# Modulation products of a two-block transformer kernel on four column positions at once

## The reference

```
c_act = silu(c)                                   # 1 x 2048
for l in range(2):
    mod = c_act @ w_mod[l] + b_mod[l]             # w_mod[l]: 2048 x 6144
    shift, scale, gate = split(mod, 3)
    h = rmsnorm(x, norm_gain[l]) * (1 + scale) + shift
    proj = h @ w_in[l]                            # 2048 x 7504
    ...                                           # sparse attention, retention, gates
    x = x + gate * (y @ w_out[l])                 # 2048 x 2048
```

## Time and profile before

| | |
|---|---|
| median of three runs | 3432.7 us |
| profiled execution | 3433.9 us, span 3432.1 us |
| TensorE matmuls | 2305.4 us busy, 67% |
| VectorE (DVE) | 1783.1 us, 52% |
| ScalarE (ACT) | 884.2 us, 26% |
| DMA | 900.92 MB, mean 262 GB/s |
| w_mod loads | 192 of 512 KB, median 4.6 us from issue to landing |
| modulation matmuls | 768, mean 671 ns, from 15.4 to 700.4 us |
| first piece of layer 0, last gate group stored | 153.85 us, 700.07 us |
| first piece of layer 1 | 824.58 us |

### The profile page before, as it was taken

One profiled execution on the slowest core, in us unless ns is written; L12 is line 12 of the kernel. 1 busy time (PEld: TensorE's weight loads), 2 busy tenths in 40 slices (PEclk: granted clock), 3 DMA queues, 4 the chain that ended last, 5 costly groups with the idle time before them and its releaser, 6 DMA issues.

```text
span 3432.1 us, 29641 instructions
## 1 busy us (share of the span) xinstructions
PE 2305.4 (67%) x11714; PEld 1506.5 (44%) x11714; DVE 1783.1 (52%) x2738; ACT 884.2 (26%) x1322; POOL 724.6 (21%) x552
## 2 busy tenths in 40 slices
PE   5899999988999878998998888123322322232235
PEld 1366666567878666665666678100000000000001
DVE  2324545655566765433234557955655565555440
ACT  1133443343455344354354442000000000000000
POOL 1000000000000000000000002555555555555552
PEclk9899999999999999999999999656666666666567
DMA  7787776744655443533332467799999999999998
GB/s 244 255 270 233 246 229 214 239 158 139 181 160 150 146 132 118 150 114 105 92 99 85 142 184 283 305 421 421 421 422 421 421 422 422 422 421 422 421 422 348
DMA packets 268133, 900.92 MB, mean 262 GB/s; under 512 B 20358, under 2 KB 45196, under 8 KB 201548
## 3 DMA queue, kind: packets, MB, share of 16 engines
q0 software_dynamic: 75776, 545.73, 38.6%
q1 hardware_dynamic: 191776, 352.69, 33.0%
q10 hardware_dynamic: 444, 0.61, 0.1%
HBM read 894.77 MB, written 2.10 MB: 261 GB/s over the span
## 4 chain that ended last, share of the span: by engine, by line
PE 55%; DMA 28%; DVE 10%; ACT 3%; issue 2%; POOL 1%; SPq 0%; DVEq 0%; POOLq 0%; ACTq 0%
PE pp L1635 47%; DMA late<-in_peer_v,MI 9%; PE tp L1635 6%; DMA P<-in_peer_v,MI 4%; DMA ring<-in_peer_v,MI 4%; DMA x<-in_peer_v,MI 4%; DMA ring<-in_w_mod 2%; DVE wL L997 2%; DMA SY<-in_peer_v,MI 2%; PE tp L1638 2%; DVE P L1050 2%; DMA ring<-in_peer_w_query 1%; DMA ring<-in_w_in 1%; ACT wH L518 1%; DVE P L1594 0%
## 5 line engine op out<-in xcount | busy, mean ns | idle before, releaser
L997 DVE TENSOR_TENSOR wL<-ring,wH 128x1024 fp32r<-128x1024 f32 (+3 forms) x504 | 581.6, 1160 | 649.7 <-ACT wH L518 648.9
L1635 PE MATMUL pp<-wH,hH 128*128 128x512 f32 (+3 forms) x1888 | 752.0, 398 | 52.6 <-issue 17.9
L1635 PE MATMUL pp<-wL,hH 128*128 128x512 f32 (+3 forms) x1888 | 719.6, 381 | 0.0
L1635 PE MATMUL pp<-wH,hL 128*128 128x512 f32 (+3 forms) x1888 | 719.5, 381 | 0.0
L518 ACT ACTIVATE wH<-ring 128x1024 fp32r<-128x1024 f32 (+3 forms) x504 | 503.5, 1005 | 551.3 <-PE pp L1635 340.1
L1635 PEld LDWEIGHTS pp<-wH,hH 128*128 128x128 f32 x1888 | 360.2, 191 | 263.9 <-issue 149.0
L1635 PE MATMUL pp<-late,S 128*32 128x512 f32 x736 | 229.7, 893 | 296.7 <-DMA P<-in_peer_v,MI 76.0
L1635 PEld LDWEIGHTS pp<-wH,hL 128*128 128x128 f32 x1888 | 360.0, 191 | 64.2
L1635 PEld LDWEIGHTS pp<-wL,hH 128*128 128x128 f32 x1888 | 360.9, 191 | 54.6 <-issue 0.5
L1635 PE MATMUL pp<-P,S 128*32 128x512 f32 x376 | 265.3, 872 | 146.8 <-DMA x<-in_peer_v,MI 73.8
L1635 PE MATMUL pp<-x,S 128*32 128x512 f32 x376 | 165.6, 874 | 223.8 <-DMA ring<-in_peer_v,MI 223.8
(11 more groups left out here) (296 smaller groups left out, 3020.4 us busy)
## 6 DMA issues: line engine op xcount, KB each, us to landing
ring<-in_w_in SPq DMA_DIRECT2D x288, 512.0 KB, 3.8
ring<-in_w_mod SPq DMA_DIRECT2D x192, 512.0 KB, 4.6
ring<-in_w_out SPq DMA_DIRECT2D x96, 512.0 KB, 4.6
ring<-in_w_in SPq DMA_DIRECT2D x48, 368.0 KB, 3.8
ring<-in_peer_w_query SPq DMA_DIRECT2D x32, 512.0 KB, 4.8
ring<-in_w_in SPq DMA_DIRECT2D x24, 344.0 KB, 3.1
ring<-in_w_in SPq DMA_DIRECT2D x16, 256.0 KB, 3.6
U<-in_dm POOLq DMA_DIRECT2D x8, 384.0 KB, 4.3
```

What stands on the lines that cost most here:

```text
L997: tt(lo, raw, hi.bitcast(F32), ALU.subtract).then_inc(*tick("dve_lo", *names))
L1635: return e.matmul(o, l, r, start=start, stop=stop, skip_group_check=skip)
```

## The change

- A w_mod load is 128 rows by 1024 columns (512 KB as before, rows of 4 KB). TensorE makes four products of 256 columns of it, one for each column position; the position stands for a quarter of the columns, and all sixteen row blocks are added up in place. A block of 1024 columns takes sixteen loads.
- The loads have buffers of their own. In the lead (loads 0 to 63) there are eight, in `late`; after it (64 to 191) two, in the columns of `P` that hold the gates later. Eight, or two, loads are issued ahead; load m + 8 or m + 2 waits for the use of m. Load 64 also waits until the last chunk of the hidden state is turned. ACT's store of the first gate group waits for the use of load 191. The ring serves the other weights alone.
- The sums: ACT copies 256 columns, TensorE turns them with two products against a four-column `ROW`, and DVE adds the bias straight from PSUM; `mrow` is gone. It is done once for 1024 columns, twelve times in all instead of 24.
- The M lane of the 128 later loads is opened after group 0 of layer 0 instead of ahead of it, and its rate in the projections is 1.5 steps a piece instead of 1.0: one and two steps in turn.

```diff
-    cw[:, ROW] = (i % 32) == 0
+    cw[:, ROW:ROW + 4] = i[:, None] == 32 * np.arange(4)[None, :]
...
-    yield "open", "M", "mods", 0, 0, 8
+    yield "open", "M", "mods", 0, 4
...
-    yield "open", "M", "mods", 0, 8, 12
-    yield "open", "M", "mods", 1, 0, 8
-    yield "open", "M", "mods", 1, 8, 12
...
         def after_in(n):
+            if n == 0 and l == 0:
+                yield "open", "M", "mods", 4, 12
...
-        yield from project(2 * l, after_in, lambda n: (0.7 if n < 14 else 1.0, 0.6, 1.0))
+        yield from project(2 * l, after_in, lambda n: (0.7 if n < 14 else 1.0, 0.6, 1.5))
...
+        mod_in = [*[late[:, 1024 * b:1024 * b + 1024] for b in range(8)], P[:, 0, GA:GA + 1024], P[:, 1, GA:GA + 1024]]
...
+        def mod_slot(m):
+
+            if m < 64:
+                return m % 8, m - 8 if m >= 8 else None
+            return 8 + m % 2, m - 2 if m >= 66 else None
...
-            def mods(l, g0, g1):
-                for g in range(g0, g1):
-                    for pc in range(8):
-                        load(I["w_mod"][l, pc * 256:(pc + 1) * 256, g * 512:(g + 1) * 512]
-                             .rearrange("(k p) n -> p k n", p=128), 2, 512)
-                        if pc < 7:
-                            yield
-                    yield
+            def mod_load(m):
+                block, k = m // 16, m % 16
+                l, c0 = block // 6, block % 6 * 1024
+                b, before = mod_slot(m)
+                if before is not None:
+                    w.wait_ge(*at("mod used", before))
+                if m == 64:
+                    w.wait_ge(*at("chunk", 0, 3))
+                e.dma_start(mod_in[b], I["w_mod"][l, k * 128:(k + 1) * 128, c0:c0 + 1024]).then_inc(
+                    *landed(f"mod_in{b}", ("mod", m)))
+
+            def mods(b0, b1):
+                first, last, depth = 16 * b0, 16 * b1, 2 if b0 else 8
+                for m in range(first, first + depth):
+                    mod_load(m)
+                for m in range(first, last):
+                    if m + depth < last:
+                        mod_load(m + depth)
+                    if m % 16 < 15:
+                        yield
+                    elif m + 1 < last:
+                        yield
+                yield
...
+                            elif p == 0:
+                                w.wait_ge(*at("mod used", 191))
...
-                    act(msum[:, :], side_bank[:, :], ACT.Copy).then_inc(*tick("act_side", ("side out", s)))
+                    act(msum[:, 0:256], side_bank[:, 0:256], ACT.Copy).then_inc(*tick("act_side", ("side out", n)))
...
-                    copy(mrow[:, 4 * g:4 * g + 4], tp[u % 2][:, 0:4]).then_inc(*tick("dve_side", ("pair free", u)))
...
+                    tt(mc.rearrange("p (g b) -> p b g", g=4), heads(tp[u % 2][:, 0:8], 2),
+                       bcol[:, l * 48 + k0:l * 48 + k0 + 8].rearrange("p (g b) -> p b g", g=4), ALU.add).then_inc(
+                        *tick("dve_side", ("pair free", u)))
...
-                        for k in range(2):
-                            kk = 2 * pc + k
-                            o = 32 * (kk % 4)
-                            m = mm(side_bank[o:o + 32, :], cact[:, kk:kk + 1].to_broadcast([128, 32]), wv[:, k, :], kk < 4, kk >= 12)
...
+                        w.wait_ge(*at("mod", m))
+                        for g in range(4):
+                            z = mm(side_bank[32 * g:32 * g + 32, 0:256], cact[:, k:k + 1].to_broadcast([128, 32]),
+                                   wv[:, 256 * g:256 * g + 256], k == 0, k == 15)
+                        z.then_inc(*tick("pe_side", ("mod used", m), *([("side", n)] if k == 15 else [])))
...
-                    for b in range(4):
-                        m = mm(pr[:, b:b + 1], msum[:, b * 128:(b + 1) * 128], CW[:, ROW:ROW + 1], True, True)
+                    for b in range(2):
+                        z = mm(pr[:, 4 * b:4 * b + 4], msum[:, b * 128:(b + 1) * 128], CW[:, ROW:ROW + 4], True, True)
```

More of the change, by code:

```diff
@@ L334, in mixer_peer_program @@
         mcol = sb("mcol", [128, 2, 48])
-        mrow = sb("mrow", [128, 48])
         msum = sb("msum", [128, 512])
@@ L361, in mixer_peer_program @@
                      "dve_lo", "dve_stored", "dve_x", "dve_y", "dve_h", "dve_side",
-                     "const_in", "pos_in", "x_in", "meta_in", "forget_in", "ffn_in", "decay_in", "turned_in", "out_done",
+                     *[f"mod_in{i}" for i in range(10)], "const_in", "pos_in", "x_in", "meta_in", "forget_in", "ffn_in", "decay_in", "turned_in", "out_done",
                      *[f"ring_in{i}" for i in range(NS)], *[f"expert_in{i}" for i in range(NG)]):
@@ L617, in tables, with mods @@
                             yield
[L619 to L623, removed]
-                            yield
[L625 to L628, removed]
-                    act(msum[:, :], side_bank[:, :], ACT.Copy).then_inc(*tick("act_side", ("side out", s)))
+            def mods(b0, b1):
+                for block in range(b0, b1):
+                    for k in range(16):
+                        if k < 15:
+                            yield
+                    n = next(side)
+                    w.wait_ge(*at("side", n))
+                    if n:
+                        w.wait_ge(*at("side read", n - 1))
+                    act(msum[:, 0:256], side_bank[:, 0:256], ACT.Copy).then_inc(*tick("act_side", ("side out", n)))
                     yield
@@ L1149, in mods @@
                     u = next(turn)
+                    l, k0 = block // 6, block % 6 * 8
+                    mc = mcol[:, l, k0:k0 + 8]
                     w.wait_ge(*at("turned", u))
-                    copy(mrow[:, 4 * g:4 * g + 4], tp[u % 2][:, 0:4]).then_inc(*tick("dve_side", ("pair free", u)))
[L1152 to L1160, removed]
+                    tt(mc.rearrange("p (g b) -> p b g", g=4), heads(tp[u % 2][:, 0:8], 2),
+                       bcol[:, l * 48 + k0:l * 48 + k0 + 8].rearrange("p (g b) -> p b g", g=4), ALU.add).then_inc(
+                        *tick("dve_side", ("pair free", u)))
+                    if block % 6 in (2, 3):
+                        w.wait_ge(*now("dve_side"))
+                        ts(mc, mc, 1.0, None, ALU.add, None).then_inc(*tick("dve_side"))
+                        w.wait_ge(*now("dve_side"))
+                        tt(mc, mc, col("norm_gain", 16 * l + k0 - 16, 8), ALU.mult).then_inc(*tick("dve_side"))
             def meta_sum(p, n):
@@ L1730, in tables, with mods @@
                             yield
[L1732 to L1739, removed]
-                            w.wait_ge(*at("c ready"))
-                            if s:
-                                w.wait_ge(*at("side out", s - 1))
-                        for k in range(2):
-                            kk = 2 * pc + k
-                            o = 32 * (kk % 4)
-                            m = mm(side_bank[o:o + 32, :], cact[:, kk:kk + 1].to_broadcast([128, 32]), wv[:, k, :], kk < 4, kk >= 12)
-                        m.then_inc(*tick("pe_side", ("ring used", r), *([("side", s)] if pc == 7 else [])))
-                        if pc < 7:
+            def mods(b0, b1):
+                for block in range(b0, b1):
+                    n = next(side)
+                    for k in range(16):
+                        m = 16 * block + k
+                        wv = mod_in[mod_slot(m)[0]]
+                        if k == 0:
+                            w.wait_ge(*at("c ready"))
+                            if n:
+                                w.wait_ge(*at("side out", n - 1))
+                        w.wait_ge(*at("mod", m))
[3 more added lines that the diff above has]
+                        z.then_inc(*tick("pe_side", ("mod used", m), *([("side", n)] if k == 15 else [])))
+                        if k < 15:
@@ L1749, in mods @@
                             yield
                     yield
-                    w.wait_ge(*at("side out", s))
+                    w.wait_ge(*at("side out", n))
                     pr, u = pair()
-                    for b in range(4):
-                        m = mm(pr[:, b:b + 1], msum[:, b * 128:(b + 1) * 128], CW[:, ROW:ROW + 1], True, True)
-                    m.then_inc(*tick("pe_turned", ("turned", u), ("side read", s)))
+                    for b in range(2):
+                        z = mm(pr[:, 4 * b:4 * b + 4], msum[:, b * 128:(b + 1) * 128], CW[:, ROW:ROW + 4], True, True)
@@ L1757, in meta_sum @@
+                    z.then_inc(*tick("pe_turned", ("turned", u), ("side read", n)))
             def meta_sum(p, n):
```

## The result

The changed kernel took 3461.6 us (median of four runs, 3460.98 to 3466.65) against 3432.6 us (four runs): a ratio of 1.0073 [1.0060, 1.0087], 0.73% slower. 3391 us was predicted, in a range of 3357 to 3422 us and with a chance of 0.08 for slower. The prediction is wrong in sign, and the time lies outside its range. The profiled execution took 3460.98 us with a span of 3459.1 us, 27.0 us above the span before.

The account below looks back on a forecast made before the run. The lead was taken as bound by a ring too short for the landing time, layer 0's projection by TensorE. Terms -31 - 1 - 5 + 19 - 24 = -42 us took 3433.9 to 3391 us, range 3357 to 3422.

Parts of the forecast that it names:

- The product: TensorE queue: one w_mod load's four-position product costs 0.77 us alone instead of 1.20, 0.43 as second of two.
- The lead: First 64 w_mod loads: eight buffers make DMA engines set the pace at 380 GB/s, x 4 us later; -31 us.
- Turn, group 0, groups 12 to 15: Turn to first piece -1 us; group 0 -5 and groups 12 to 15 -24, as layer 1 without products takes.
- The waits on w_mod: Groups 1 to 11: TensorE waits for loads in two buffers, 27 plus 15 us, 42 in all.
- the product c: Second of two back-to-back products in a two-piece period, following a and b; its load, issued at a's use, comes late.
- The time without waits: Groups 1 to 11: layer 1's 261.9 us plus products and turns of the sums, 350 us against 372.8.
- The landing: SP's w_mod loads: 4.4 us to land by the trace, against a skill-based estimate of 3.2 us.
- So 350 + 42 = 392 us: Groups 1 to 11: work without waits plus waits on w_mod, +19 us against 372.8; bounds -23 and +51.
- The late w_in: Groups 1 to 11: w_in queued behind SP's wait, ready at 7.3 us, needed after 7.7 or more; nothing priced.
- B: Groups 1 to 11: two buffers make landing the bound, 5.7 us or more; stretch +98, 3470 us; chance 0.08.
- A: Groups 1 to 11: loads land in time, under 3.5 us; stretch 350 us, total 3349 us; chance 0.15.
- C: TensorE products: four positions don't help, a load still costs 1.20 us; stretch +57, total 3429 us; chance 0.04.

Follow-up runs that it names:

- experiment 4: Changed kernel, but loads 64 to 191 go through the four ring slots, one a piece, opened ahead of group 0: 3354.8 us, ratio 0.9753.
- Experiment 6: Changed kernel with six buffers for loads 64 to 149 and SP waiting for the product three back: 3359.8 us, ratio 0.9782.
- experiment 7: Changed kernel, still two buffers, but SP waits for the product three back instead of its own step's: 3407.0 us, ratio 0.9911.
- Experiments 1 and 2: Changed kernel with SP's wait one product back (3425.9 us); changed kernel with six buffers for loads 64 to 149, SP's wait unchanged (3442.8 us).
- 9: The kernel of experiment 4 with the load of x issued first in GpSimd's queue, ahead of the constants: 3352.1 us, ratio 0.9748.
- experiment 5: Changed kernel's products and sums, but all 192 loads go through the four ring slots as before the change: 3376.4 us, ratio 0.9824.

## Why the prediction was wrong

**What held.** *The product.* "A single product in the queue then costs 0.77 us": measured 0.75 (experiment 4), with nothing left for an overhead that grows as the columns shrink. The estimate from the Trainium skill, TensorEngine Tiling (Array Packing), section Performance Considerations, would have made it 0.82 us; no such cost is seen. *The lead.* x 3.9 us later (4 said); then 410 GB/s, above my 380 and inside its bounds, at 1.02 DMA share; in exchange a load takes 9.2 us to land, with eight under way. *Turn, group 0, groups 12 to 15* came as derived from the twin. *The waits on w_mod.* 42 us were priced, at the product c, and the matmul queue waits 42.0 us, 36.5 of them at c. That the sums agree so well is partly luck: groups 1 to 3 have 19.6 us of it where 27 were priced, the wide groups 22.4 where 15 were. *The time without waits.* Experiment 6, the same schedule with most of the limits gone, keeps TensorE busy for 348 us at a granted clock of 0.99, against 350 in the sum. *The landing.* The Trainium skill, DMA: Bandwidth & Descriptors, section Anatomy of one DMA, has a fit for GpSimd-issued transfers that gives an estimate of 3.2 us for 512 KB. No w_mod load of the two kernels, all issued by SP, reached it; the shortest took 3.6 us.

**The step that failed: "So 350 + 42 = 392 us" for groups 1 to 11, which leaves two terms at nothing.** It was 477. In the change's own profile the stretch is 348 us of work as experiment 6 has it, 43 us by which the work became longer, 42 us of waits on w_mod, and 43 us of waits for ACT and DVE. The first and the third are the two terms of the sum. The other two are its error.

1. *The late w_in: "It is late only if DVE or ACT is held up; ACT's and DVE's lane work behind it slips along, which the tensor engine then waits for."* The sentence names the mechanism, and the sum gives it nothing. I had worked out the slack of the late w_in for the piece that needs it, 7.3 against 7.7 us, and taken 0.4 us of it as cover. What I left out is what ACT does in order behind its wait for w_in: 43 us of TensorE's idle time, which become 3 us when SP no longer stands in that wait (7). Experiments 1 and 2 show it from both sides: less SP order, more waiting on w_mod, and 40 us gained; hardly any waiting on w_mod, SP's order kept, and only 16 gained.
2. *No price for the clock.* The stretch's 2370 matmuls keep TensorE busy for 348 us in 6, at a granted clock of 0.99; 370 in 7, at 0.95; 392 after the change, at 0.90. The idle time is 20, 55 and 86 us in the three. Of the 708 weight loads for `hH` there, 4, 68 and 103 took over 280 ns, where 188 is usual: so the engine ran at the lower of its two levels, 1.2 instead of 2.4 GHz, for more of the work. 43 of the 109 us between 6 and the change are work that became longer, about 22 in each of the two steps. The Trainium skill, TensorE: Matmul & The Clock Gate, section Part 1 (The HAM clock gate), says that the clock that is let through depends on how busy the engine has been recently; the trace agrees.

By the corners, the same 127 us over 350 are 18 without either limit in full (6), 57 for the two buffers (7 against 6) and 52 for SP's order (the change against 7), with the slower work in each of the last two. In 6, 10.6 us of the 18 are waits on w_mod, and all thirteen are for loads 150 to 191, which still have two buffers there. So the two buffers cost more than the 42 us of waits say, 57 us by the corners and 47 by the medians, with 22 us of slower work in it; alone they would have left the change faster than the kernel before.

Three readings of the prediction were off without bearing on the sign. The 42.6 us of the earlier trace rows are of the weight-load queue; the matmul queue was idle for 97.00 - 74.72 = 22.3 us there. SP's issue in the earlier trace rows follows the product's end by 403.33 - 403.29 = 0.04 us, not 0.11. And the range used bounds narrower than those of its parts; with theirs it would have ended at 3434 us, still below 3461.6.

**The rivals.** *B* was nearest: +98 for the stretch and 3470 us in all, against +104 and 3461.6, but by luck. Its landing of 5.7 us or more was not there (median 4.3), nor its 84 us or more of waits on w_mod (42.0), and its mechanism, two buffers alone, is experiment 7: 3407 us, faster than before. It needed SP's order to lose. *A* failed at the landing: 4.3 us, not under 3.5. *C* is refuted by 0.75 us. Of the signs that I had named as proof of a wrong prediction, neither was there as I had put it: the waits on w_mod stayed under 84 us, and the direct waits on remainders are 1.5 us in the matmul queue (9.8 for PEld). The late w_in showed in the waits behind it, on ACT's copies and stores and on the attention steps.

The best version is the ring behind a lead of eight buffers (4, 9): 2.5% faster than before, about 3% faster than the change. Its margin comes from the lead and the product alone; the later loads go where they went. Experiment 6 is within 0.3% of it.

## What to carry to other kernels

A queue that issues in order and waits for a buffer's reader delays everything queued behind that wait; price it by what stands behind the delayed transfer on every engine that works in order, not by the one instruction that reads it. When loads get their own buffers, count how many products back the issuer's wait reaches: three back with two buffers beat none back with six (3407 against 3443 us). And price a stall of TensorE with what the lower clock takes from the work beside it: here 109 us were 66 of idleness and 43 of slower matmuls.

## What the runs showed of the hardware

- With eight w_mod loads of 4 KB rows under way, the DMA engines moved 410 GB/s at 1.02 share and a load took 9.2 us to land; with four slots (experiment 5) 320 GB/s at 0.92 share and 5.5 us. Twice as many under way bought 28% more rate, the rest went into the landing time. The granted clock of the same window was 0.89 and 0.61.
- 4 KB rows against 2 KB rows at four slots, both from 45 to 105 us: 320 GB/s at 0.92 share (5) and 272 at 0.82 (before), with the same median landing of 5.5 us. The products differ too, so the gain is not the rows' alone for certain.
- 86 us of idleness of TensorE in 477, spread over many gaps (the longest 8.6 us, those on w_mod at most 2.7), went with a granted clock of 0.90; 55 us in 425, no gap over 3.1 us, with 0.95 (7); 20 us in 368 with 0.99 (6).
